# Expert value product in eight pieces of 64 rows by 32 columns, activations in four column quarters

## What is computed

```python
def block(args):
    xb, ib, gb = args
    h = jnp.einsum('td,ted->te', xb, u_tab[ib], preferred_element_type=jnp.float32)
    act = jax.nn.gelu(h, approximate=False) * gb
    return jnp.einsum('te,ted->td', act.astype(xb.dtype), v_tab[ib])
```

## Time and profile before

| | |
|---|---|
| runs | 3987.51, 3988.76, 3993.89 us; median 3988.76 |
| profiled execution, first to last instruction | 3986.4 us (its own device time is not listed beside it) |
| PE / DVE / ACT / POOL busy | 75 / 62 / 39 / 32% |
| mean granted TensorE clock | 0.849 of 2.4 GHz |
| memory traffic | 1261 MB, mean 316 GB/s |
| two expert stages with the gathers running | 720 to 2124 us and 2531 to 3948 us |

### The profile page before, as it was taken

The page is one execution under the profiler, slowest core; times in us unless marked ns, Lnnn a source line. Parts: engine busy times, 40 slices in busy tenths (PEclk is TensorE's granted clock), DMA queues, the critical chain, the costliest instruction groups (busy, mean ns, idle before and its releaser), DMA issues. The chain is left out here.

```text
span 3986.4 us, 45941 instructions
## 1 busy us (share of the span) xinstructions
PE 3005.8 (75%) x14557; PEld 1439.4 (36%) x14557; DVE 2474.6 (62%) x6084; ACT 1535.0 (39%) x4402; POOL 1289.7 (32%) x1172
## 2 busy tenths in 40 slices
PE   7997888777666677768757798776777876666666
PEld 6886775322212122223313575322232222222221
DVE  2665443676676667767773343476677677667675
ACT  2352121444343344446432221344544444334332
POOL 0004330444434333333441110233334344334433
PEclk9998788988778788888878898888888988787778
DMA  2211002999999999999996453799999999999998
GB/s 89 73 51 55 13 13 71 404 420 416 420 414 418 405 397 387 411 366 384 402 421 244 165 204 144 291 375 390 381 375 415 405 404 421 413 420 413 411 421 334
DMA packets 234350, 1261.33 MB, mean 316 GB/s; under 512 B 32008, under 2 KB 71952, under 8 KB 97552
## 3 DMA queue, kind: packets, MB, share of 16 engines
q0 software_dynamic: 153600, 1133.58, 69.8%
q1 hardware_dynamic: 80528, 125.08, 9.1%
HBM read 1244.25 MB, written 14.19 MB: 316 GB/s over the span
## 5 line engine op out<-in xcount | busy, mean ns | idle before, releaser
L1951 PE MATMUL acc<-ring,diag 128*64 128x512 f32 x4096 | 1339.0, 751 | 751.3 <-ACT diag L1650 748.9
L1569 POOL DMA_INDIRECT ring<-in_uv,idx x1024 | 1119.1, 1093 | 1895.3 <-PE acc L1951 1635.2
L1761 DVE SCALAR_TENSOR_TENSOR ring<-ring,rep 128x1024 f32<-128x1024 f32 x1024 | 1230.6, 1221 | 368.9 <-DMA ring<-in_uv,idx 309.3
L1951 PEld LDWEIGHTS acc<-ring,diag 128*64 128x64 f32 x4096 | 250.3, 158 | 1494.2 <-ACT diag L1650 1317.8
L1642 ACT ACTIVATE hg<-hs 128x1 f32<-128x1 f32 x1024 | 203.7, 199 | 1141.1 <-DVE ring L1761 1139.1
L1650 ACT ACTIVATE diag<-const,hgg 128x64 f32<-128x64 f32 x1024 | 356.4, 348 | 33.4
L1646 ACT ACTIVATE hgg<-hg,weigh_by 128x1 f32<-128x1 f32 x1024 | 302.0, 295 | 33.2
L1883 PE MATMUL big<-xnT,w 128*128 128x264 f32 (+1 forms) x960 | 297.1, 435 | 0.0
L1883 PEld LDWEIGHTS big<-xnT,w 128*128 128x128 f32 x960 | 174.8, 203 | 185.0 <-issue 166.4
L298 PE MATMUL acc<-xnT,w 128*128 128x260 f32 x1024 | 230.2, 386 | 0.7 <-ACT inp L419 0.7
L298 PEld LDWEIGHTS acc<-xnT,w 128*128 128x128 f32 x1024 | 196.3, 192 | 38.4 <-issue 7.5
(11 more groups left out here) (571 smaller groups left out, 4057.7 us busy)
## 6 DMA issues: line engine op xcount, KB each, us to landing
w<-in_w_peer SPq DMA_DIRECT2D x64, 512.0 KB
w<-in_w_gdn SPq DMA_DIRECT2D x32, 512.0 KB, 3.6
ring<-in_uv,idx POOLq DMA_INDIRECT x1024, 12.3
wo<-in_w_mla_out SPq DMA_DIRECT2D x8, 1024.0 KB, 11.5
wo<-in_w_uq SPq DMA_DIRECT2D x8, 768.0 KB, 14.2
out_ssm_s<-states SPq DMA_DIRECT2D x4, 1024.0 KB, 5.1
wo<-in_w_gdn_out SPq DMA_DIRECT2D x4, 1024.0 KB, 8.2
sk<-in_keys SPq DMA_DIRECT2D x64, 64.0 KB
```

The source lines that it names most:

```text
L1569: pool.indirect_dma_start(out=ring[:, c % RING, :], out_offset=None, in_=uv, in_offset=bass.IndirectOffsetOnAxis(ap=idx[u % 2][:, c:c + 1] ...
L1761: dve.scalar_tensor_tensor(ring[:, c % RING, 0:D], ring[:, c % RING, 0:D], 1.0, rep[:, 2 * a + c // RING, :], ALU.mult, ALU.mult, accum_ou ...
L1951: last = pe.matmul(acc[i][rows(j), :], diag[:, r, :], ring[:, r, D + HALF * j:D + HALF * j + HALF], start=r == 0, stop=r == RING - 1)
```

## The change

Activations (`core.x`, `xn`, `gain`, the accumulators) are laid out in four column quarters instead of two halves: partitions 32j to 32j+31 hold columns 256j to 256j+255 of 32 rows, and a group's second 32 rows lie beside the first in the free dimension (`side(e)`). The 128 gathered rows of a step are laid out (`lay`) so that partitions 0 to 63 serve 32 tokens and 64 to 127 the other 32. The diagonal is therefore 128 by 32, and the value product becomes eight products: four column quarters times two row halves, each with 256 streamed. The two row halves write different banks. One PSUM tile `acc` [128, 2, 512] holds both token groups of a unit; DVE adds all of it after the first dot of the next unit, and the next unit's first product waits for both adds. Squares, row scaling and transposed copies of a group are done in two pieces; the gain comes in four DMAs instead of two.

```diff
+LO = 32
+QD = D // 4
+def side(e):
+
+    return slice(QD * e, QD * e + QD)
+
+
+def quarters(xnT, bank, first, n):
+
+    pieces = []
+    for e in range(2 if n > LO else 1):
+        m = min(n, LO)
+        pieces.append((xnT[:, :, first + LO * e:first + LO * e + m].rearrange("p (q k) c -> p q k c", q=4),
+                       bank[:, 2 * e:2 * e + 2, :].rearrange("p k (q c) -> p q k c", q=4)[:, :, :, 0:m]))
+    return pieces
...
-                for j in range(2):
-                    sp.dma_start(gain[TG * j:TG * j + TG, :], gain_row[:, HALF * j:HALF * j + HALF].to_broadcast([TG, HALF])).then_inc(s["gain"], 16)
+                for j in range(4):
+                    sp.dma_start(gain[LO * j:LO * j + LO, :], gain_row[:, QD * j:QD * j + QD].to_broadcast([LO, QD])).then_inc(s["gain"], 16)
...
-                        act.activation(junk, core.x[:, base + g, :], ACT.Square, accum_out=stat[:, 0, g:g + 1]).then_inc(s["sum"], 1)
+                        for e in range(2):
+                            last = act.activation(junk[:, side(e)], core.x[:, base + g, side(e)], ACT.Square, accum_out=stat[:, 0, g, e:e + 1])
+                        last.then_inc(s["sum"], 1)
...
-                        dve.scalar_tensor_tensor(xn[:, (g - 1) % 4, :], core.x[:, base + g - 1, :], stat[:, 2, g - 1:g], gain, ALU.mult, ALU.mult).then_inc(s["row"], 1)
+                        for e in range(2):
+                            last = dve.scalar_tensor_tensor(xn[:, (g - 1) % 4, side(e)], core.x[:, base + g - 1, side(e)], stat[:, 2, g - 1, e:e + 1], gain, ALU.mult, ALU.mult)
+                        last.then_inc(s["row"], 1)
...
-                        act.activation(diag[:, c % RING, :], core.const[:, C_PAIR, 0:TG], ACT.Copy, scale=hgg[a][:, c:c + 1]).then_inc(s["diag"], 1)
+                        act.activation(diag[:, c % RING, :], core.const[:, C_PAIR, 0:LO], ACT.Copy, scale=hgg[a][:, c:c + 1]).then_inc(s["diag"], 1)
...
-                def add(u, i):
-
-                    g = 2 * tile_of(u) + i
-                    after(dve, at("pv", u, RING * i + RING))
-                    dve.tensor_tensor(core.x[:, g, :], acc[i][:, :], core.x[:, g, :], ALU.add).then_inc(s["added"], 1)
+                def add(u):
+
+                    g = 2 * tile_of(u)
+                    after(dve, at("pv", u, TOPK))
+                    for e in range(2):
+                        mine = core.x[:, g:g + 2, side(e)]
+                        dve.tensor_tensor(mine, acc[:, e, :].rearrange("p (i c) -> p i c", i=2), mine, ALU.add).then_inc(s["added"], 1)
...
+                        if c == 0 and u:
+                            add(u - 1)
...
-                        if c == 9:
-                            add(u, 0)
-                        if c == 2 and u:
-                            add(u - 1, 1)
...
                         for g in groups:
-                            lhs = os[:, kk, :] if g == GS else oT[:, kk, TG * g:TG * g + TG]
-                            for j in range(2):
-                                last = pe.matmul(summed(g)[rows(j), :], lhs, wo[:, kk, column(j)], start=kk == 0, stop=kk == KD - 1)
+                            for e in sides(g):
+                                n = TG * g + LO * e
+                                lhs = os[:, kk, :] if g == GS else oT[:, kk, n:n + LO]
+                                for j in range(4):
+                                    last = pe.matmul(summed(g)[quarter(j), side(e)], lhs, wo[:, kk, side(j)], start=kk == 0 and e == 0, stop=kk == KD - 1, skip_group_check=True)
...
                     for i in range(2):
-                        for r in range(2):
-                            last = pe.matmul(pR[rows(r), e, RING * i:RING * i + RING], core.const[:, C_ID, rows(i)], src[:, RING * r:RING * r + RING], start=True, stop=True)
+                        for half in range(2):
+                            for r in range(2):
+                                last = pe.matmul(pR[quarter(2 * half + r), e, RING * i:RING * i + RING], core.const[:, C_ID, quarter(2 * i + half)], src[:, RING * r:RING * r + RING], start=True, stop=True)
...
-                        if r == 0:
-                            after(pe, at("added", u - 1, i + 1) if u else (s["o_added"], 4))
-                        for j in range(2):
-                            last = pe.matmul(acc[i][rows(j), :], diag[:, r, :], ring[:, r, D + HALF * j:D + HALF * j + HALF], start=r == 0, stop=r == RING - 1)
+                        if c == 0:
+                            after(pe, at("added", u, 0) if u else (s["o_added"], 4))
+                        for j in range(4):
+                            for e in range(2):
+                                last = pe.matmul(acc[quarter(j), e, side(i)], diag[rows(e), r, :], ring[rows(e), r, D + QD * j:D + QD * j + QD], start=r == 0, stop=r == RING - 1)
...
                 for b in range(NS):
-                    for j in range(2):
-                        last = pe.matmul(acc[0][rows(j), :], sac[:, b, :], ring[:, b, D + HALF * j:D + HALF * j + HALF], start=b == 0, stop=b == NS - 1)
+                    for j in range(4):
+                        last = pe.matmul(acc[quarter(j), 0, 0:QD], sac[:, b, :], ring[:, b, D + QD * j:D + QD * j + QD], start=b == 0, stop=b == NS - 1)
```

More of the change, by code:

```diff
@@ L142, in norm @@
     count = GROUPS - base
-    with Marks(core, "norm", gain=32, sum=1, paired=1, mean=1, root=1, inv=1, row=1, turned=1, copied=1, copied2=1) as s, ExitStack() as ctx:
-        stat = core.sbuf(ctx, "stat", [P, 3, count])
+    with Marks(core, "norm", gain=64, sum=1, paired=1, mean=1, root=1, inv=1, row=1, turned=1, copied=1, copied2=1) as s, ExitStack() as ctx:
+        stat = core.sbuf(ctx, "stat", [P, 3, count, 2])
         pair = [core.psum(ctx, "pair", [P, HALF]) for _ in range(2)]
@@ L151, in across @@
         def across(g):
[L152 to L153 removed]
+            return quarters(xnT, bank[g % 2], *here(g))
         with nc.Block() as block:
@@ L1510, in across, with sides @@
         def across(g):
-            first, n = here(g)
-            return xnT[:, :, first:first + n].rearrange("p (j k) c -> p k j c", j=2), turned_bank(g).rearrange("p k (j c) -> p k j c", j=2)[:, :, :, 0:n]
+            return quarters(xnT, turned_bank(g), *here(g))
+        def sides(g):
+            return range(1 if g == GS else 2)
         def here(g):
@@ L1528, in _ @@
                     sp.dma_start(wo[:, 2 * i:2 * i + 2, :], wd[:, 2 * i:2 * i + 2, :]).then_inc(s[f"o_w{i}"], 16)
-                for j in range(2):
-                    sp.dma_start(gain[rows(j), :], core.i["norm_ffn"][layer:layer + 1, column(j)].to_broadcast([TG, HALF])).then_inc(s["gain"], 16)
+                for j in range(4):
+                    sp.dma_start(gain[quarter(j), :], core.i["norm_ffn"][layer:layer + 1, side(j)].to_broadcast([LO, QD])).then_inc(s["gain"], 16)
                 def load(hh, p):
@@ L1590, in spread_over @@
                         after(act, at("q_made", H - 2, 2))
-                    act.activation(*across(g), ACT.Copy).then_inc(s["copied"], 1)
+                    for to, come in across(g):
+                        last = act.activation(to, come, ACT.Copy)
+                    last.then_inc(s["copied"], 1)
                 def first_queries(t):
@@ L1696, in row @@
                         after(dve, at("rep_made", (g - 4) // 2, 4))
-                    dve.scalar_tensor_tensor(normed(g), core.x[:, g, :], stat[:, 2, g:g + 1], gain[:, :], ALU.mult, ALU.mult).then_inc(s["row"], 1)
+                    for e in range(2):
+                        last = dve.scalar_tensor_tensor(normed(g)[:, side(e)], core.x[:, g, side(e)], stat[:, 2, g, e:e + 1], gain[:, :], ALU.mult, ALU.mult)
+                    last.then_inc(s["row"], 1)
                 def spread_over(g):
@@ L1892, in repeat @@
                         after(pe, at("q_out", H - 1, 2))
-                    pe.matmul(pq[:, :], core.const[:, C_REP + i % 2, :], normed(g), start=True, stop=True).then_inc(s["rep_made"], 1)
+                    for j in range(2):
+                        for e in range(2):
+                            last = pe.matmul(pq[rows(e), side(j)], core.const[:, C_REP + i % 2, rows(j)], normed(g)[:, side(e)], start=True, stop=True)
+                    last.then_inc(s["rep_made"], 1)
                 def score(v):
@@ L1915, in sample_row @@
                         after(pe, mla.at("out", H, 0))
-                    for j in range(2):
-                        n = TG * j + b
-                        last = pe.matmul(big[b % 2][:, column(j)], core.const[:, C_ID, n:n + 1].to_broadcast([P, P]), xns[:, :], start=True, stop=True)
+                    for j in range(4):
+                        n = LO * j + b
+                        last = pe.matmul(big[b % 2][:, side(j)], core.const[:, C_ID, n:n + 1].to_broadcast([P, P]), xns[:, 0:QD], start=True, stop=True)
                     last.then_inc(s["rowed"], 1)
```

112 lines of the change are left out of this document (65 added, 47 removed).

## The result

The changed kernel takes 3934.8 us (median of 4 runs, 3930.4 to 3938.3) against 3991.3 (4 runs) beside it: ratio 0.9858, 95% interval [0.9843, 0.9874], 1.4% faster. Two later sets of runs of it gave 0.9843 and 0.9855.

The account below looks back on a forecast made before the run. DMA traffic was taken to bound both expert stages, PE mattering only in dips. Dips -24, layer ends -7.5, work outside the loops +4.5 and code +4.2 gave -22.8 us: 3966 us from 3988.8, range 3941 to 3995.

Parts of the forecast that it names:

- what bounds the kernel now: Both expert stages: memory traffic sets their time, full at DMA share 1.02 and 421 GB/s; starvation in dips costs 44 us.
- The rest of the sum: Whole kernel: dips -24, layer ends -7.5, work outside the loops +4.5, code +4.2, together -22.8 us.
- Dips: Expert loops, where DMA engines briefly run dry: shorter value products win back 24 of 44 us, bounds 0 and 57.
- The step's time: Value product on PE: a step takes 0.46 us instead of 0.86 at full clock, total busy 700 to 850 us.
- Rival A: Expert-loop dips: DVE bursts and attention transfers cause them all, not PE; 3990 us, no change; chance 0.18.
- Rival E: PE clock: with less work, full clock is granted less often, eating part of the 24 us; counted in main case's range.
- Ends of the layers: Sample product and its add at each layer's end: shorter, -7.5 us over two layers, bounds -6.5 and -9.
- Heads: Outside the loops: norm scaling and squares in pieces, gain DMAs, expert-stage heads add +4.5 us, bounds 2 and 9.
- Code: Instruction fetch over the DMA engines: 30,000 more instructions, 1.75 MB, add 4.2 us, bounds 0 and 8.
- Rivals B and D: Value product: row halves take turns, 3990 us, chance 0.05; or records run one after another, 5370 us, chance 0.02.
- rival C: Unit heads: DVE waits for the previous unit's last product, holding everything behind it; up to 4032 us, chance 0.11.

Follow-up runs that it names:

- the run with 32 bytes: Changed kernel with 32 unused bytes per partition ahead of the ring, putting the ring 32 bytes off a multiple of 64: 3962.8 us, ratio 0.9938 to the kernel before.
- the adds-only run: Kernel before with both adds of a unit moved behind the first dot of the next unit, layout and products unchanged: 3987.9 us, ratio 0.9990.

## Why the prediction was wrong

The whole in one table of ratios:

```
                              512 columns               256 columns, rest left out   the change
ring off a multiple of 256    1.0002  1.0005  1.0000    0.9925                       0.9938  0.9921
ring on a multiple of 256     0.9946  0.9936            0.9836                       0.9858  0.9843  0.9855
```

- **The step that failed** is in "what bounds the kernel now": "In a quiet stretch the DMA share is 1.02 at 421 GB/s, which I take as full", and from it "nothing but DMA counts" in the quiet stretches. That DMA alone counts there held. What failed was taking its rate as given. The change moved the ring by 1952 bytes, onto a multiple of 256; each row's packet got 1.8% shorter (316.1 to 310.5 ns) and some 25 us went. That is shown from both sides: 20 and 22 us on the kernel before, 25 us on the changed one beside itself (and 28 to 34 for the run with 32 bytes, against sets that did not run beside it). The sum had no term for it, and no rival spoke of it, though the change resizes `os`, `gain` and `stat` ahead of the ring.
- **The rest of the sum** was -22.8 us. With the ring held off the multiple, the change gives 26 us and 33 us in two sets of runs, 3963 and 3956 us, both inside the range. Half the columns on the kernel before gave 3962 us with none of the other edits (ratio 0.9925, against 0.9938 and 0.9921), so layout, ends, heads and code together come to nothing that these runs can tell; 1.2 us were forecast for them.
- **Dips.** Forecast -24 of 44. Half the columns alone, with none of the other edits, gives -27, and the changed kernel without its ring's luck, after taking out the ends, heads and code below, about -26 to -35. The mechanism is shown: with half the columns the traffic rises from 389 to 399 GB/s in the woven stretch of layer 0, and in the quiet ones it goes from 414 to 416 and from 416 to 414. The 24 us were a guess inside 0 to 57 from shares rounded to hundredths, so that they came out a little low and no further off is partly luck. Rival A is out.
- **The step's time.** Forecast 0.46 us of streaming. At the full clock that is about right: from the first start to the last end a step takes 0.67 us at the median in the woven stretches (1.08 before). In the quiet ones the median is 1.11 (1.08 before; the means are 0.95 and 1.4), because most steps there now run at half clock, in two batches 0.43 us apart. Busy time was thus 913 us and not 700 to 850. Row halves and column quarters run side by side; that the same number of columns in 64x32 tiles or in 128x64 tiles costs PE the same is shown by 913 against 916 us.
- **Rival E** came further than allowed for: the clock fell from 0.80 to 0.64 in the second half of layer 1's stage (0.70 to 0.75 was forecast) and from 0.87 to 0.77 in its first half. In the quiet stretches that took back PE time and not kernel time: with the ring off the multiple they run at 416 GB/s at a clock of 0.64 as they did at 0.80. What it costs in the woven stretches no run separates.
- **Ends of the layers.** -7.5 forecast. At the end of layer 1 the sample product fell from 8.78 to 5.35 us and its add from 0.69 to 0.43, 3.7 us in all; layer 0's product fell from 9.97 to 6.38. (The prediction's own terms, 4.3 less four times 0.21, make 3.45 for a product and not the 3.3 that it writes; 3.43 is what came.) From the last dot to the end the kernel takes 36.8 us in place of 39.8, so 3.0 arrived at the end of layer 1.
- **Heads.** +4.5 forecast. The first norm's last row ends 1.6 us later (36.66 against 35.02 us); from the projection to the first dot layer 0 takes 50.5 to 51.7 us (51.1 before) and layer 1 51.5 to 51.7 (50.8 to 51.1). The second norm's rows take 9.6 us in place of 8.9. Together that is 2 to 3 us.
- **Code.** 3.67 + 0.98 = 4.65 MB, 1.97 more than before, against 1.75 forecast; by an estimate 4.6 us at 424 GB/s. No run separates it; it is only argued.
- **Rivals B and D** are refuted by the records, rival C by the adds-only run (no slower, and a wait of 68.5 us before the adds in place of 117.2).

## What to carry to other kernels

When a kernel is bound by its gathers, the rate of a full DMA stretch is not to be taken as given (here 413 to 418 GB/s with the ring off a multiple of 256 and 419 to 424 with it on one): print where each large DMA target begins in its partition before and after an edit, and compare the duration of one packet, not only the share. An edit that resizes a small buffer can be worth nearly as much by that as by what it was made for (some 25 us against 26 to 33 here), and a pad of 96 bytes gave a third of this change's gain and no other edit. An engine that is off the path for most of the time still pays where others share it, and how much is told better by leaving out half of its work than by adding up idle shares.

## What was not expected of the hardware

- Packets of 8192 bytes into SBUF take 309 ns each when the target begins on a multiple of 256 bytes, and 309 to 321 ns (mean 315 to 316) at 32, 128, 160 and 192 past one. How far past does not matter within what these runs can tell: two runs at 160 past give 316.1 and 315.6. The Trainium skill, DMA: Bandwidth & Descriptors (How a descriptor splits into AXI transactions), says, speaking of reads, that a transaction starts on a 256-byte boundary, so that a transfer which does not pays for bytes that it fetches and doesn't use. These runs agree that 256 is the step. By its beats of 32 bytes, an estimate, the row would cost 257 in place of 256 at 32 past the boundary and 262 at 192 past it, 0.4% and 2.3%; measured are 1.8% and 1.5%, so the growth with the offset is not seen here. Why the packets spread, and whether the side that is read behaves likewise, stays open.
- A step of half the columns is at the median no shorter in a quiet stretch: 1.11 us with a granted clock of 0.64, against 1.08 with 0.80 before (3200 to 3900 us).
